# Swapping two projections of a hybrid encoder layer: layer norm ahead of the attention loop, spatial mixing into heads 1 and 2

## The reference, cut to what matters

```
proj = rmsnorm(x) @ w_in            # latent q, latent kv, rotary key, then u (512 columns) and v (512)
o_mla = 8 heads of latent attention (64 + 32 rotary dims), 512 x 512 scores each
z = gelu(h_sg); u, v = z[..., :512], z[..., 512:]
v = layernorm(v, ln_g, ln_b)                              # over the 512 columns of v
mixed = einsum('hij,bcjhd->bcihd', w_s, v) + b_s          # inside chunks of 128 tokens, 8 groups of 64 columns
o_sg = u * mixed
x = x + concat(rmsnorm(o_mla), rmsnorm(o_sg)) @ w_out
```

## Time and profile before

| what | us |
|---|---|
| runs | 1603.77, 1604.22, 1606.22 |
| median | 1604.22 |
| span of the profiled execution | 1605.4 |
| TensorE busy | 1487.2 (93%) |
| VectorE busy | 780.2 (49%) |
| ScalarE busy | 759.9 (47%) |
| GpSimd busy | 698.3 (43%) |

### The profile page before, as it was taken

One profiled execution on the slowest core, in us unless ns is written; L12 is line 12 of the kernel. 1 busy time (PEld: TensorE's weight loads), 2 busy tenths in 40 slices (PEclk: granted clock), 3 DMA queues, 4 the chain that ended last, 5 costly groups with the idle time before them and its releaser, 6 DMA issues.

```text
span 1605.4 us, 20864 instructions
## 1 busy us (share of the span) xinstructions
PE 1487.2 (93%) x6846; PEld 1204.2 (75%) x6846; DVE 780.2 (49%) x1264; ACT 759.9 (47%) x1187; POOL 698.3 (43%) x327
## 2 busy tenths in 40 slices
PE   4988889997999999999999787999889999999995
PEld 3765568876888888888877565798778888888883
DVE  4538767815265430355153786783423654114543
ACT  5666745536344441344356676564534444224431
POOL 3365415840434454334546453386123534544350
PEclk9998999999999999999999899999999999999997
DMA  4310013530223332223322101244111233322221
GB/s 169 113 66 27 14 53 120 183 105 1 92 66 105 105 105 95 77 91 105 122 80 92 53 14 40 91 147 156 41 53 66 94 102 105 112 98 81 90 79 53
DMA packets 39048, 138.91 MB, mean 87 GB/s; under 512 B 4848, under 2 KB 5104, under 8 KB 38704
## 3 DMA queue, kind: packets, MB, share of 16 engines
q1 hardware_dynamic: 37440, 134.23, 25.0%
q10 hardware_dynamic: 1520, 3.52, 0.7%
HBM read 135.64 MB, written 2.10 MB: 86 GB/s over the span
## 4 chain that ended last, share of the span: by engine, by line
PE 49%; issue 29%; POOL 13%; DVE 5%; ACT 3%; POOLq 0%; DVEq 0%; ACTq 0%
PE ps L1341 16%; PE ps L1342 16%; PE ps L1343 16%; POOL w_lo L367 11%; DVE small L1038 1%; POOL arena L387 1%; DVE work L1134 1%; ACT arena L595 0%; ACT work L587 0%; ACT arena L581 0%; DVE small L1039 0%; ACT h_hi L595 0%; DVE work L1132 0%; POOL work L382 0%; POOL work L381 0%
## 5 line engine op out<-in xcount | busy, mean ns | idle before, releaser
L367 POOL TENSOR_TENSOR w_lo<-raw,w_hi 128x1024 fp32r<-128x1024 f32 x248 | 603.2, 2450 | 769.4 <-ACT w_hi L469 768.0
L1341 PE MATMUL ps<-h_hi,w_hi 128*128 128x512 f32 (+2 forms) x1040 | 408.5, 393 | 25.3 <-POOL w_lo L367 22.3
L469 ACT ACTIVATE w_hi<-raw 128x1024 fp32r<-128x1024 f32 x248 | 255.7, 1054 | 323.7 <-PE ps L1343 322.7
L1342 PE MATMUL ps<-h_lo,w_hi 128*128 128x512 f32 (+2 forms) x1040 | 404.3, 389 | 0.0
L1343 PE MATMUL ps<-h_hi,w_lo 128*128 128x512 f32 (+2 forms) x1040 | 404.1, 389 | 0.0
L1341 PE MATMUL ps<-arena,w_hi 128*128 128x512 f32 (+2 forms) x656 | 245.3, 374 | 8.1 <-DVE arena L1032 4.1
L1341 PEld LDWEIGHTS ps<-h_hi,w_hi 128*128 128x128 f32 (+1 forms) x1040 | 195.5, 188 | 69.6 <-issue 22.5
L1342 PE MATMUL ps<-arena,w_hi 128*128 128x512 f32 (+2 forms) x656 | 243.2, 371 | 0.0
L1343 PE MATMUL ps<-arena,w_lo 128*128 128x512 f32 (+2 forms) x656 | 243.2, 371 | 0.0
L1343 PEld LDWEIGHTS ps<-h_hi,w_lo 128*128 128x128 f32 (+1 forms) x1040 | 195.5, 188 | 41.2
L1342 PEld LDWEIGHTS ps<-h_lo,w_hi 128*128 128x128 f32 (+1 forms) x1040 | 195.6, 188 | 40.8 <-issue 1.0
(11 more groups left out here) (175 smaller groups left out, 1889.1 us busy)
## 6 DMA issues: line engine op xcount, KB each, us to landing
raw<-blocks_d SPq DMA_DIRECT2D x248, 512.0 KB, 3.3
x<-xT_d SPq DMA_DIRECT2D x4, 512.0 KB, 8.6
work<-memT_d ACTq DMA_DIRECT2D x2, 1024.0 KB, 4.7
outT_d<-work SPq DMA_DIRECT2D x8, 256.0 KB, 2.2
work<-ln_d ACTq DMA_DIRECT2D x2, 512.0 KB, 3.6
par<-par_d ACTq DMA_DIRECT2D x2, 113.5 KB, 2.0
work<-pos_d ACTq DMA_DIRECT2D x1, 128.0 KB, 6.9
mix_g<-par_d ACTq DMA_DIRECT2D x2, 4.0 KB, 6.6
```

Of the source, the lines that this page charges most:

```text
L367: gp.tensor_tensor(w_lo[:, b % SPLIT, :], raw[:, b % RAW, :], w_hi[:, b % SPLIT, :].bitcast(F32), ALU.subtract).then_inc(lo_done.sem, 1)
L469: act.activation(w_hi[:, b % SPLIT, :], raw[:, r, :], ACT.Copy).then_inc(hi_done.sem, 1)
L1341: pe.matmul(out, a_hi, b_hi, start=first, stop=False)
L1342: pe.matmul(out, a_hi, b_lo, start=False, stop=False)
```

## The change

The two token-major projections change places, in the blocks' order and in the program: v is projected first, u after the first heads' q and k. The statistics, root and layer norm of v move from heads 0 to 3 of the loop to the stretch ahead of it, on VectorE around the first two maxima; ScalarE's high halves of v stand behind the gelus of u, GpSimd's low halves ahead of its loop. The mixing moves from heads 4 and 5 to heads 1 and 2, the gated statistics from head 6 to head 3, the second root and the scaling from (7, 0) to (4, 0), and the four turns of the gated tiles from head 7 and behind it to heads 5 and 6. The weight block of the mixing comes one place earlier, and one split of ScalarE moves from (7, 0) to (5, 2) with the next one behind it.

```diff
-B_U = B_LAT + 4
-B_WV = B_U + 4
-B_V = B_WV + 2
-B_HEAD = (B_WV + 1, B_V + 4, B_V + 5, B_V + 7)
-B_WS = B_V + 6
-B_OUT = B_V + 8
+B_V = B_LAT + 4
+B_WV = B_V + 4
+B_U = B_WV + 2
+B_HEAD = (B_WV + 1, B_U + 4, B_U + 6, B_U + 7)
+B_WS = B_U + 5
+B_OUT = B_U + 8
...
-MIX_STEPS = ((4, 1), (4, 3), (5, 0), (5, 2))
-GATED_STEPS = ((6, 0), (6, 1), (6, 2), (6, 3))
+MIX_STEPS = ((1, 0), (1, 2), (2, 0), (2, 2))
+GATED_STEPS = ((3, 0), (3, 1), (3, 2), (3, 3))
+TURN_STEPS = ((5, 0), (5, 2), (6, 0), (6, 2))
-STAT_STEPS = ((0, 1), (0, 2), (0, 3), (1, 0))
-NORM_STEPS = ((1, 1), (1, 3), (2, 1), (3, 1))
-SPLIT_STEPS = ((1, 2), (2, 0), (2, 2), (3, 2))
...
@@ gpsimd
-                for b in range(B_V + AHEAD, B_V + 7):
+                for b in range(B_U + AHEAD, B_U + 7):
                     low(b)
+                need(lo_done, B_U + 7)
+                for t in range(TT):
+                    gate_low(t)
+                need(svl_done, TT)
                 for h in range(HEADS):
...
-                        if h in (2, 3):
-                            need(roped, h + 3)
-                            gate_low(2 * h - 4)
-                            gate_low(2 * h - 3)
-                            need(svl_done, 2 * h - 2)
...
@@ scalar
                     rotated(h)
-                act.preload_act_table_set("natural_log_exp_and_others")
+                small_root(2)
                 exps(0)
                 exps(1)
-                for b in range(B_V + 1, B_V + 4):
+                for b in range(B_U + 1, B_U + 4):
                     ahead(b)
                 for t in range(TT):
...
-                    act.activation(vt[:, t, :], ps[BA[t]][:, :], ACT.Gelu_apprx_tanh, scale=rs_tok[:, t:t + 1])\
-                        .then_inc(vg_done.sem, 1)
+                    act.activation(u[:, t, :], ps[BA[t]][:, :], ACT.Gelu_apprx_tanh, scale=rs_tok[:, t:t + 1])\
+                        .then_inc(u_done.sem, 1)
+                for t in range(TT):
+                    need(vn_done, t + 1)
+                    act.activation(sv_hi[:, t, :], vt[:, t, :], ACT.Copy).then_inc(svh_done.sem, 1)
                 act.preload_act_table_set("natural_log_exp_and_others")
...
-                    if t == 2 and h in (2, 4, 6):
-                        ahead(B_V + 4 + h // 2)
-                    if (h, t) == (7, 0):
-                        ahead(B_OUT)
+                    if t == 2 and h in (2, 4, 5, 6):
+                        ahead((B_U + 5, B_U + 6, B_U + 7, B_OUT)[(2, 4, 5, 6).index(h)])
...
-                    if (h, t) == STAT_STEPS[-1]:
-                        small_root(2)
                     if (h, t) == GATED_STEPS[-1]:
                         small_root(3)
-                    if (h, t) == (7, 2):
-                        gate_turned(0)
-                    if (h, t) in SPLIT_STEPS:
-                        g = SPLIT_STEPS.index((h, t))
-                        need(vn_done, g + 1)
-                        act.activation(sv_hi[:, g, :], vt[:, g, :], ACT.Copy).then_inc(svh_done.sem, 1)
-                gate_turned(1)
+                    if (h, t) in TURN_STEPS:
+                        gate_turned(TURN_STEPS.index((h, t)))
                 copy_sums(HEADS - 1)
-                gate_turned(2)
                 square_output(3)
-                gate_turned(3)
...
@@ vector
+                for t in range(TT):
+                    need(vg_done, t + 1)
+                    statistics(vt, t)
+                dve.tensor_scalar(sm_v, mv[:, :, 1], EPS, None, ALU.add).then_inc(s_v.sem, 1)
+                small_root(2)
                 amax(0)
                 amax(1)
+                need(ln_in, 16)
+                for t in range(TT):
+                    link(dve.tensor_scalar(vt[:, t, :], vt[:, t, :], mv[:, t, 0:1], sm_t[:, t:t + 1],
+                                           ALU.subtract, ALU.mult))
+                    link(dve.tensor_tensor(vt[:, t, :], vt[:, t, :], ln_gb[:, 0, :], ALU.mult))
+                    dve.tensor_tensor(vt[:, t, :], vt[:, t, :], ln_gb[:, 1, :], ALU.add).then_inc(vn_done.sem, 1)
                 for i in range(HEADS * TT):
...
-                    if (h, t) == (7, 0):
+                    if (h, t) == (4, 0):
                         small_root(3)
...
-                    if (h, t) == (7, 2):
-                        gate_turned(0)
+                    if (h, t) in TURN_STEPS:
+                        gate_turned(TURN_STEPS.index((h, t)))
                     turned_lo(i)
                 recip_sums(HEADS - 1)
-                gate_turned(1)
-                gate_turned(2)
                 attended(HEADS - 1)
                 add_square(3)
-                gate_turned(3)
...
@@ tensor
-                project_tokens(B_U, BA, h_hi, h_lo, lambda k: None, between=latent_sums)
+                project_tokens(B_V, BA, h_hi, h_lo, lambda k: None, between=latent_sums)
...
-                need(u_done, 4)
-                project_tokens(B_V, BA, h_hi, h_lo, lambda k: None, between=first_scores, tile_mm=v_mm)
-                need(vg_done, 4)
+                need(vg_done, 4)
+                project_tokens(B_U, BA, h_hi, h_lo, lambda k: None, between=first_scores, tile_mm=u_mm)
+                need(u_done, 4)
...
-                    if h == HEADS - 1 and t % 2:
-                        turn_gated(t // 2)
+                    if (h, t) in TURN_STEPS:
+                        turn_gated(TURN_STEPS.index((h, t)))
                 attend(HEADS - 1)
                 spread_sums(HEADS - 1)
-                turn_gated(2)
                 def mixed(k):
-                    if k == 5:
-                        turn_gated(3)
```

More of the change, by code:

```diff
@@ L249, in encoder_program @@
         svl_done = sig("svl_done", 4)
-        v_mm = sig("v_mm", TT - 1)
+        u_mm = sig("u_mm", TT - 1)
         mq_mm = sig("mq_mm", 6)
@@ L393, in gate_low @@
                         .then_inc(svl_done.sem, 1)
-                lows(0, B_V + AHEAD)
-                need(lo_done, B_V + AHEAD)
+                lows(0, B_U + AHEAD)
+                need(lo_done, B_U + AHEAD)
                 for h in range(2):
@@ L402, in layer @@
                 need(pel_done, 2)
-                for b in range(B_V + AHEAD, B_V + 7):
+                for b in range(B_U + AHEAD, B_U + 7):
                     low(b)
+                need(lo_done, B_U + 7)
+                for t in range(TT):
+                    gate_low(t)
+                need(svl_done, TT)
                 for h in range(HEADS):
                     if h % 2 == 1:
-                        low(B_V + 7 + h // 2)
+                        low(B_U + 7 + h // 2)
                     if h + 2 < HEADS:
-                        need(lo_done, B_V + 7 + (h + 1) // 2)
+                        need(lo_done, B_U + 7 + (h + 1) // 2)
                         rotate(h + 2)
-                        if h in (2, 3):
-                            need(roped, h + 3)
-                            gate_low(2 * h - 4)
-                            gate_low(2 * h - 3)
-                            need(svl_done, 2 * h - 2)
                         rotated_low(h + 2)
@@ L534, in layer @@
                 squares(NKV, lambda t: lat_kv, lambda t: need(lat_done, 1), acc_t=sq[:, 1, :])
-                ahead(B_U)
+                ahead(B_V)
                 need(kpe_ready, 1)
@@ L538, in layer @@
                     act.activation(k_hi[64:96, p, :], rot[64:96, 2, :], ACT.Copy).then_inc(kpe_hi.sem, 1)
-                ahead(B_U + 1)
+                ahead(B_V + 1)
                 small_root(1)
@@ L542, in layer @@
                 his(NKV, lambda t: ckv_hi[:, t, :])
-                ahead(B_U + 2)
+                ahead(B_V + 2)
                 need(nlo_done, TILE0[NKV] + 1)
@@ L546, in layer @@
                               ln_d[bass.ds(l, 1), :].to_broadcast([P, 2 * SG])).then_inc(ln_in.sem, 16)
-                ahead(B_U + 3)
+                ahead(B_V + 3)
                 ahead(B_WV)
@@ L557, in layer @@
                 for t in range(TT):
-                    act.activation(u[:, t, :], ps[BA[t]][:, :], ACT.Gelu_apprx_tanh, scale=rs_tok[:, t:t + 1])\
-                        .then_inc(u_done.sem, 1)
+                    act.activation(vt[:, t, :], ps[BA[t]][:, :], ACT.Gelu_apprx_tanh, scale=rs_tok[:, t:t + 1])\
+                        .then_inc(vg_done.sem, 1)
                 ahead(B_HEAD[0])
@@ L624, in layer @@
                     if h == 1:
-                        ahead(B_V)
+                        ahead(B_U)
                     rotated(h)
-                act.preload_act_table_set("natural_log_exp_and_others")
+                small_root(2)
                 exps(0)
                 exps(1)
-                for b in range(B_V + 1, B_V + 4):
+                for b in range(B_U + 1, B_U + 4):
                     ahead(b)
@@ L634, in layer @@
                     if t < TT - 1:
[L635 removed]
+                        need(u_mm, t + 1)
                     else:
[L637 to L639 removed]
+                        block_used(B_U + 3)
```

(4 more changed lines are left out.)

16 lines of the change are left out of this document (removed).

## The result

The changed kernel takes 1618.67 us, the median of four runs (1617.64 to 1622.84). The kernel before, run beside it, takes 1603.99. The ratio is 1.009, with a 95% interval from 1.0077 to 1.0102: slower by 14.7 us. The forecast was 1624, between 1608 and 1632.

The account below looks back on a forecast made before the run. It took the loop's ring of ScalarE and VectorE, 2.96 us a step, as the limit, not TensorE. Terms of 13.0 + 0.1 - 3.0 = 10.1 us a layer, 20.2 in all, gave 1624 us, between 1608 and 1632.

Parts of the forecast that it names:

- Part 1: Ahead of the loop: norm of v held under GpSimd's operations, exponential 2 near 120 instead of 107 us; +13.0 us a layer.
- The tie at the end: Tile 3's last norm product, issued within 0.2 us of a GpSimd low half, might go first: 1.9 us less over both layers.
- Part 2: Attention loop, exponential 2 to 31: new excess 18.8 us against 18.7 before, so +0.1 us a layer.
- The largest term: Gate turns at (5,0), (5,2), (6,0), (6,2): VectorE's subtraction queues behind a wait for ScalarE's copy; 10.0 us together.
- The mix steps at t = 2: Mixing moved to heads 1 and 2: steps (1,2) and (2,2) cost 1.16 us each, the others fit; 2.3 us.
- Gated statistics with the root's load: Steps (3,0) to (3,3): VectorE fits 1.9 us into 1.4, and a table load stands at (3,3); 1.5 us.
- (4, 0): Head 4, first query tile: second root and four scalings on VectorE beside GpSimd's rotated low part; 3.0 us.
- Plain steps: Loop steps without added work: 0.5 us kept of the earlier excess and 1.5 of the later; regular step 2.96.
- Part 3: Behind the loop: 1.5 us less to head 7's attention, 1.5 less to the resumed output projection; -3.0 us a layer.
- The hold is not there: Rival, ahead of head 0 and at (4,0): VectorE is not held by GpSimd; 1602 or 1599 us; chance 0.10.
- The turns ride in ScalarE's room: Rival, gate turns: only VectorE's 0.75 us of each is paid; 7.0 a layer less, 1610 us; chance 0.15.
- TensorE's clock: Rival, heads 0 and 1, waits at heads 5 and 6: TensorE at 1.2 GHz; +4 us a layer, 1632; chance 0.08.

Follow-up runs that it names:

- Run 1: Changed kernel, with GpSimd's last three weight subtractions ahead of the loop waiting for the layer norm of v: 1605.93 us, ratio 1.0003 to the kernel before.
- Run 4: Changed kernel, with the exponential table loaded ahead of ScalarE's four high halves of v instead of behind them: 1618.0 us, ratio 1.0088 to the kernel before.
- run 2: Changed kernel, with VectorE's part of each of the four gate turns one step later: 1608.36 us, ratio 1.0017 to the kernel before.
- run 3: Changed kernel, with the four gate turns back in head 7 and behind it, as in the kernel before: 1613.59 us, ratio 1.0061 to that kernel.
- run 9: On run 6, five small float32 matmuls with unused results at (6, 0), (6, 1) and (6, 2), filling TensorE's idle time: 1584.18 us, ratio 0.9871.
- run 5: Changed kernel with the edits of run 1 and run 2 together: 1592.91 us, ratio 0.9917 to the kernel before.
- run 6: On run 5, the four scalings of the gated tiles spread one to a step of head 4: 1586.68 us, ratio 0.989 to the kernel before.
- run 8: On run 5, two large float32 matmuls with overwritten results ahead of the scores at (6, 2): 1597.96 us, ratio 0.9952 to the kernel before.

## Why the prediction was right

**Part 1, ahead of the loop: right, +12.2 for +13.0.** The chain came as written. The root was held to the end of GpSimd's first subtraction, the maxima moved back, and the norm of tiles 1 to 3 went operation by operation under GpSimd's. Run 1 shows the hold on the norm to be the cause of 7.75 of the 12.2 us. As many operations were held as forecast, six, though not the same ones: I had the tensor-scalar of tile 1 as the first. It was issued just before the subtraction and ran free (0.54), and the tensor-scalar of tile 2 was held in its stead. The small overestimate is in their price: three operations under weight subtractions took 8.1 us, where I had 8.6. The tie at the end, for the last product of tile 3, GpSimd won: its low half had begun at 114.54, and the product issued at 115.02 took 1.63 us. The Trainium skill (SBUF — State Buffer, section "Who interferes with whom") says that whoever issues first gets the shared port for the whole instruction, which these rows bear out: that low half, begun under the product before, took 1.56 us, and the last one, with no product beside it, 1.26.

The remaining 4.5 us were named too, but not parted by a run: the hold of the root (2.02 us, which run 1 leaves in place), and gelus, copies and a table load behind TensorE's last block. Run 4 shows that the load itself is worth 1.1 us a layer.

**Part 2, inside the loop: -2.5 and -2.0 for +0.1.** The largest term looks right to a tenth, and that is partly luck. The turn steps exceed 2.96 by 2.03, 2.65, 2.02 and 3.24, 9.9 us for the forecast 10.0 (9.3 in layer 1). At (5, 0) and (6, 0) it is the wait as I had it: run 2 takes both away. But run 3, without the turns in the loop, is only 7.5 and 5.5 us shorter there. At (6, 2) it still exceeds a plain step by 2.2 and 2.6 us, part of which is the clock, as run 9 shows. In the kernel before the step at (6, 2) is long too (5.80 and 4.49 us), and I took that excess off with the gated statistics. So two errors cancel: I booked 3.0 us there as the turn's, of which run 3 shows 1.1 and 0.0 to be so, and removed an excess that is there again in run 3. The same turns also cost 3.4 and 2.0 us in their old place behind the loop. What was mis-sized openly is the rest:
- The mix steps at t = 2 cost 0.99 and 1.31 (1.16 in layer 1), forecast 1.16 each. Right.
- Gated statistics with the root's load: 1.2 over the four steps of head 3, forecast 1.5. Nearly right.
- (4, 0): 2.17, forecast 3.0. The scalings met the rotated low part once, as I had it (2.68 us for four), but the hold was 0.7 us, not the full 1.3.
- Plain steps: 0.5 + 1.5 forecast, 0.6 found. I had filled this with a remainder of the step list before. Why that remainder did not stay was not tried. Slow matmuls are not the reason for most of it: 0.85 us lay in the steps to exponentials 20 to 24 of the kernel before, where the clock was granted at 1.00.

**Part 3, behind the loop: half right.** The 1.5 us up to the resumed projection came (1.46 and 1.47). Of the other 1.5, only 0.6 came. Stretches of the changed kernel behind the last steps show why:

```profile
218.00:220.00 2.00, 0.53 (x5) 0.32 (x4) 0.92 (x2) 1.05 (x3) 0.00 (x0) 1.00 0.00 0
...
222.00:224.00 2.00, 2.00 (x6) 1.07 (x5) 1.29 (x2) 1.48 (x4) 0.00 (x0) 0.50 0.00 0
```

TensorE has 0.53 us of work in 218 to 220, and in 222 to 224 it runs at the 1.2 GHz level. The attention product of head 6 is stretched, the transposes of step 31 come at 224.74, and VectorE waits 1.67 us for that product. I had counted this chain at full clock. In runs 2, 5 and 6 it has the same instructions and takes 4.80 us, with the clock at 1.00, as in run 2:

```profile
215.00:217.00 2.00, 2.00 (x10) 1.22 (x9) 1.01 (x2) 2.00 (x6) 0.00 (x0) 1.00 0.00 0
```

Just ahead of the attention product TensorE waits 1.47 us in both kernels, so that wait alone does not say whether the clock falls.

**The rivals.** "The hold is not there" is refuted by the rows and by run 1. "The turns ride in ScalarE's room" is refuted by the step list; run 2 shows that they would, with the wait one step later. "TensorE's clock" named heads 0 and 1 and the waits at heads 5 and 6. At head 0 it was wrong: TensorE has nothing to do for 6.4 us ahead of exponential 2, its clock is granted at 0.50 from 118 to 128 us, and the steps to exponentials 3 to 5 are 2.96, 3.08 and 2.96 all the same, since the ring has room for it. At (6, 2) it was right in kind, and behind the loop, which it did not name, the same holds: there an attention product stands in the chain. Each is worth some 1.5 us a layer (run 9, and 6.29 against 4.80). But the kernel before has slow stretches in the same places (0.50 from 195 to 201 us and from 209 to 215), so they add little to the difference.

The measured change is below the forecast by 0.8 us in part 1 and 2.4 in part 2, and above it by 1.0 in part 3: 2.2 us a layer, 4.3 in all, of the 5 us between 1624 and the median.

## What to carry to other kernels

Before work is moved into an engine's idle stretch, look at what its neighbours do in that stretch: VectorE was free ahead of the loop, but GpSimd was at work there, and each of six VectorE operations on SBUF tiles, five products and a tensor-scalar, ended only behind the GpSimd operation that ran. One wait that orders the two was worth 12.7 us. In a ring of two engines, put an engine's part of a handed-over job behind the next turn of the ring, not in front of the instruction that carries it (7.4 us a layer in run 2); and count an addition per step, not in total: four scalings in one step cost 2.2 us, one in each of four steps 0.45 in all. And before a step that came out at its forecast length is put down to the forecast cause, take the cause away: at (6, 2) most of the length stayed.

## What the runs showed that I had not expected

- The hold works both ways. GpSimd's three subtractions took 8.20 us under the norm's operations and 7.05 in run 1 without them, 0.38 us more for each.
- An idle TensorE that is given a little useless work early was faster later: five extra matmuls a layer took 1.4 and 1.6 us off a step in run 9. The same idea, applied when TensorE had been idle for 3.26 us (run 8), cost 5.
- The runs of one kernel spread by different amounts: the range is 7 us in run 2, 6 in run 5, 3.5 in run 6 and 1.7 in run 9. Differences of that size arise where no edit is. The 16 us of layer 1 shown with run 6 have the same work in each kernel; their mean clock is 0.79 in the changed kernel and run 5, 0.89 in the kernel before and 1.00 in runs 1 and 6, and from the resumed projection to the end it takes 591.5, 589.5 and 588.3 us in turn. These are the +2.0 us of the result's section; the 3 us between the two ends are as much as several of the effects measured here, which is why the layer sums, and not the medians, carry them here. The step to exponential 29 differs between the layers of one execution (5.46 and 6.29 in run 5) and does not in run 9. What decides on the clock in these places is open.
